# Half units of weight sums moved on GpSimd, rows of x loaded later, in the mixing blocks of a one-core encoder layer

## The reference

```
xn = rmsnorm(x, g);  z = xn @ w_in                 # q | k | v | x branch | gate
attn = banded attention over 64-token chunks       # q, k, v; window 128, learned sinks
lru  = gelu(gate) * scan(conv(x branch))           # gated linear recurrence over time
h    = x + concat(attn, lru) @ w_out               # end of the mixing half
y    = h + relu(rmsnorm(h) @ w_up)^2 @ w_down      # MLP, hidden width 4096
out  = rmsnorm(y)                                  # and the caches and states of k, v, conv, lru
```

## Time and profile before

| what | value |
|---|---|
| median of the runs | 2216.5 us (2215.3 to 2217.7) |
| the profiled execution, its span | 2212.88 us, 2211.1 us |
| PE, busy | 1985.6 us (90%) |
| DVE, busy | 1535.7 us (69%) |
| ACT, busy | 1014.1 us (46%) |
| POOL, busy | 500.7 us (23%) |
| DMA | 500.91 MB, mean 227 GB/s |

### The profile page before, as it was taken

The page is one execution under the profiler, slowest core; times in us unless marked ns, Lnnn a source line. Parts: engine busy times, 40 slices in busy tenths (PEclk is TensorE's granted clock), DMA queues, the critical chain, the costliest instruction groups (busy, mean ns, idle before and its releaser), DMA issues.

```text
span 2211.1 us, 34222 instructions
## 1 busy us (share of the span) xinstructions
PE 1985.6 (90%) x11669; PEld 1882.8 (85%) x11669; DVE 1535.7 (69%) x2167; ACT 1014.1 (46%) x1967; POOL 500.7 (23%) x411
## 2 busy tenths in 40 slices
PE   6779789789789669999999889999999789999994
PEld 5678578578578569999999879999999789999994
DVE  7767667667668677888887866666666766666663
ACT  5555345454454435555555544433334534434431
POOL 3436456456549230100000400100001300000000
PEclk9989899899899889999999999999999999999997
DMA  5757566666566459998998977778878677777771
GB/s 173 232 157 228 168 195 217 176 210 194 175 202 189 127 197 301 316 308 273 338 340 295 314 242 240 238 209 250 269 230 252 222 223 217 219 216 216 216 215 63
DMA packets 396538, 500.91 MB, mean 227 GB/s; under 512 B 27498, under 2 KB 301450, under 8 KB 396394
## 3 DMA queue, kind: packets, MB, share of 16 engines
q1 hardware_dynamic: 394698, 493.38, 72.1%
q0 software_dynamic: 1696, 5.67, 0.7%
HBM read 375.36 MB, written 123.68 MB: 226 GB/s over the span
## 4 chain that ended last, share of the span: by engine, by line
PE 65%; DVE 10%; issue 9%; POOL 7%; DMA 4%; ACT 3%; SPq 1%; POOLq 0%; DVEq 0%; ACTq 0%
PE results L2067 20%; PE scores_a L2067 13%; PE tail L2067 13%; PE results L1851 10%; PE aux L2067 8%; DVE w_lo L1401 2%; PE aux L1971 1%; POOL prob L961 1%; DMA s_scratch<-w_hi 1%; POOL xrow L932 1%; POOL xrow L930 1%; DVE xg_lo L1411 1%; POOL xrow L934 1%; DVE av L1560 1%; POOL xrow L936 1%
## 5 line engine op out<-in xcount | busy, mean ns | idle before, releaser
L1083 ACT ACTIVATE w_hi<-w_raw 128x512 fp32r<-128x512 f32 (+1 forms) x360 | 240.6, 690 | 394.8 <-PE results L2067 169.6
L1526 DVE TENSOR_TENSOR w_lo<-w_raw,w_hi 128x512 fp32r<-128x512 f32 (+1 forms) x360 | 292.4, 826 | 50.7 <-ACT w_hi L1083 50.5
L1851 PE MATMUL results<-xg_hi,w_hi 128*128 128x448 f32 (+1 forms) x560 | 211.4, 377 | 30.6 <-DVE w_lo L1401 21.2
L1851 PE MATMUL results<-xg_hi,w_lo 128*128 128x448 f32 (+1 forms) x560 | 201.1, 359 | 0.0
L1851 PE MATMUL results<-xg_lo,w_hi 128*128 128x448 f32 (+1 forms) x560 | 200.9, 359 | 0.0
L2067 PE MATMUL results<-hn_hi,w_hi 128*128 128x348 f32 x576 | 188.2, 327 | 13.4 <-DVE hcur L1736 7.8
L1401 DVE TENSOR_TENSOR w_lo<-raw,w_hi 128x1024 fp32r<-128x1024 f32 x110 | 158.1, 1437 | 58.8 <-ACT w_hi L1019 58.5
L1019 ACT ACTIVATE w_hi<-raw 128x1024 fp32r<-128x1024 f32 x110 | 116.2, 1056 | 162.9 <-PE results L1851 158.2
L2067 PE MATMUL results<-hn_hi,w_lo 128*128 128x348 f32 x576 | 186.5, 324 | 0.0
L2067 PE MATMUL results<-hn_lo,w_hi 128*128 128x348 f32 x576 | 186.4, 324 | 0.0
L2067 PE MATMUL scores_a<-hn_hi,w_hi 128*128 128x348 f32 x480 | 156.2, 325 | 4.7 <-DVE hn_lo L1516 2.9
(11 more groups left out here) (275 smaller groups left out, 5723.8 us busy)
## 6 DMA issues: line engine op xcount, KB each, us to landing
w_lo<-s_scratch SPq DMA_DIRECT2D x128, 512.0 KB, 4.5
w_hi<-s_scratch SPq DMA_DIRECT2D x256, 256.0 KB, 3.5
w_raw<-in_w_up SPq DMA_DIRECT2D x144, 256.0 KB, 4.6
w_raw<-in_w_down SPq DMA_DIRECT2D x144, 256.0 KB, 4.3
raw<-in_w_in SPq DMA_DIRECT2D x70, 512.0 KB, 5.0
w_raw<-s_raw SPq DMA_DIRECT2D x64, 512.0 KB, 5.5
s_scratch<-w_lo SPq DMA_DIRECT2D x64, 512.0 KB, 6.0
s_scratch<-w_hi SPq DMA_DIRECT2D x128, 256.0 KB, 6.1
```

Of the source, the lines that this page charges most:

```text
L1083: nc.scalar.activation(ring(w2_hi, u, ks[0], len(ks)), raw_slots(u, ks[0], len(ks)), ACT.Copy)\
L1526: nc.vector.tensor_tensor(w2_lo[u.s][:, PHYS[ks[0]]:PHYS[ks[0]] + len(ks), :], raw_slots(u, ks[0], len(ks)), ring(w2_hi.bitcast(F32), u, k ...
L1851: last = nc.tensor.matmul(out, wt, x(kx), start=(start and i == 0 and part == 0), stop=(stop and i == len(ks) - 1 and part == 2))
```

## The change

Two things, in the mixing blocks. In SP's loop, `load_x` for the next block moves from n = 16 to n = 18, and at that step it now comes behind `move_sums`. It holds for the first block and the three middle ones. In the middle blocks' `SUM_MADE`, half unit 9 moves from "scan" to behind the probabilities of round 0, half unit 10 from round 1 to round 2; half unit 14 moves from ahead of the adds of squares to behind the second of them, half unit 15 from behind the third to behind the fifth. No instruction is added or removed.

```diff
-            "mid": {"start": (0, 1, 2), "ix0": (3, 4), "ix1": (5, 6), "scan": (7, 8, 9), 1: (10,), 3: (11,), 5: (12,), 6: (13,),
-                    "squares": (14,), "squares3": (15,)},
+            "mid": {"start": (0, 1, 2), "ix0": (3, 4), "ix1": (5, 6), "scan": (7, 8), 0: (9,), 2: (10,), 3: (11,), 5: (12,), 6: (13,),
+                    "squares2": (14,), "squares5": (15,)},
...
-                    if nxt and q == 7:
+                    move_sums(blk, n)
+                    if nxt and q == 8:
                         sp.wait_ge(mixed, blk.before(2) + 2)
                         sp.wait_ge(freed, 2 + uses + Z1)
                         for r in range(4):
                             load_x(nxt, r)
-                    move_sums(blk, n)
...
-                make_sums(blk, "squares")
                 for c in range(1, KT):
                     add_square(blk.next(), c)
-                    if c == 3:
-                        make_sums(blk, "squares3")
+                    make_sums(blk, f"squares{c}")
```

## The result

The changed kernel takes 2178.85 us (2178.8 and 2178.9) against 2216.5: ratio 0.983, 95% interval 0.981 to 0.986, 37.7 us less. The two profiled executions (2212.88 and 2178.8 us) differ by 34.1 us: that of before lies 3.6 us under its median. What follows splits these 34.1.

What follows compares the result with a forecast made beforehand. PE, the busiest engine, was held by GpSimd's `prob`, queued behind half unit 10's late load; 36 - 1 + 3 + 7 + 0 = 45 us off the median of 2216.5 gave 2171 us, range 2157 to 2191.

Steps and rivals of the forecast that it cites:

- Half unit 10 and x: 36: Middle blocks, rounds 1 to 4: PE's wait for GpSimd's `prob` goes, 12 us a block, 36 us for three.
- the whole 12 us go: Middle blocks: the 12 us a block lost around PE's wait for `prob` all vanish, with 1.4 us to spare.
- Half unit 9: -1 and +3: Three middle blocks: half unit 9 behind round 0's `prob` costs 1 us; DVE's faster `rt` and `mix_lo` win 3.
- the first rival: Middle blocks: half unit 9 disturbs the softmax, round 1's `prob` some 2 us late; 36 us won, 2180 us; chance 0.15.
- the rival's rule: DVE with two SBUF inputs contends with GpSimd; three softmax steps could each lose an add, 0.72 us, 2.2 a block.
- The first block: +7: First block: x moved away lets a half unit's load land earlier; of 12.3 us wait 5.5 stay, 7 won, bounds 5 to 12.3.
- Cost 0, with 4 us to spare: Later issue of x: first tile lands near 429, PE needs it at 433.1, so no cost.
- x later in the middle blocks: 0: x issued at n = 18, from about 425, still lands before PE's transposition; cost 0 us.
- The fourth rival: x lands too late, behind its transposition, in all four blocks: at 450, 23 us slower, 2240 us; chance 0.02.
- The second: Rival: half unit 10 still lands late, wait moves to round 3; 21 us won, 2195 us; chance 0.08.
- The tail: 0: Middle blocks' end, half units 14 and 15 between the adds: between +3 and -1 us a block, taken as 0.
- the third rival: Middle blocks' end: adds end with the last square, each wins 3 us; 54 us in all, 2162 us; chance 0.13.

## Why the prediction held, point by point

It said 2171 us, 45 us off; 37.7 came by the medians and 34.1 in the two traces, with the range holding. The mechanism was right, and the sum 11 us too high against its own execution. By stretches of the traces, the 34.1 are: rounds 0 to 5 of three middle blocks +36.0, from round 5 to x -4.0, x to the sum +2.6, sum to round 0 -1.8, first block +3.8, last block and MLP -2.5. The last of these lies ahead of the last block's round 0 (102.0 us from its sum against 99.6); its cause stays open, since kernels whose sum is waited for took 101.3 to 103.0 there, but so did one without that wait (102.5). Behind that round the two traces agree within 0.1 us, and by the scatter of that stretch this is luck.

*Half unit 10 and x: 36.* Exactly 36.0 up to round 5. The step that failed stands behind it: "the whole 12 us go". I checked the half units next to the stall, and put half unit 13's load at nought, but not half unit 12, which stands between the `prob`s of rounds 5 and 6. Without the stall the rounds come at their own pace, and its load and adds hold round 6: 1.3 us in each block, 4.0 of the 36 given back. That this half unit does it is shown by its move, and by x at n = 17, which made its wait longer. It does not do it alone: half unit 9's new place has used up the slack, as its move back shows.

*Half unit 9: -1 and +3.* The net of 2 is not shown. The +3 is of the right kind: from `rt` to round 0 the changed kernel is 1.2 us faster than before over the three blocks, and 2.3 faster than with the half unit back. The -1 was looked for in the wrong place: round 1's `prob` transposition follows round 0's without a wait, so the first rival fell, but the rounds behind start later, and 3.0 of the 4.0 us in round 6 come back when the half unit does. DVE's step with the sink took 0.66 us beside it (0.16 with the half unit back beside the scan), one step of the three. It began at 390.22, while an add of the half unit ran, and ended with that add, at 390.88 against 390.86. So it lost 0.5 us, the rest of one add, and not the three whole adds of 0.72 each that the rival's rule allowed. The rule of the Trainium skill, "SBUF — State Buffer", "Who interferes with whom", agrees with the trace in that, and in which pairs meet, 1.09 against 1.61 and 0.16 against 0.66, while its worst case did not occur here. The price of 0.5 us an instruction was read too high from the earlier trace rows: there three instructions lost 1.06 us together.

*The first block: +7.* It gave 3.8, under the lower bound of 5, though by less than the scatter of a first block. PE's wait for `prob` fell from 12.3 to 4.1, so the rounds behind it came 7.6 to 8.5 us earlier, more than the term assumed. The step that failed is the next one: "Cost 0, with 4 us to spare" was worked out in a middle block and taken for all four. In the first, with five rounds instead of seven, x was issued at 115.73 and PE wanted it at 120.7; it came 1.2 us late and PE ran on at a granted clock of 0.70 for 5.5 us. With x a step earlier the first sum came 3.4 us sooner, which brings the term to 7.2.

*x later in the middle blocks: 0.* Right: 3.7 us to spare for the 4 forecast, and one step later there is a wait. The fourth rival falls with it. The second falls by GpSimd's rows: half unit 10 does not wait, and PE's round 3 does not either.

*The tail: 0.* Right in size and in form: `hacc` is no longer waited for, the sum is, and the matmuls run slower behind it. Taking it back changed nothing that the times or the blocks show. What I did not see is that 13 us lay there: the third rival asked whether the adds could end with the last square, and they can, once both half units stand behind them.

*The signs.* Three of those that the prediction named went against it. A wait for `prob` of over 1 us is left in the middle blocks, in round 6 and not in round 3, where it was looked for. A wait for x, which was to show that the prediction is wrong, is there in the first block. The middle blocks became 12.7, 11.9 and 8.3 us shorter, not 14 to 15. Others held: half unit 10 does not wait, x is issued 7.7 us ahead of its transposition, and a wait stands ahead of the sum in place of the one for `hacc`.

The result, 1.7% faster, lies in the case to which the chances gave 0.51, with that for over 2% close beside it at 0.47: as the text said, the forecast stood almost on the boundary.

## What to carry to other kernels

Where an engine does side work between steps of the critical chain, put that work behind the last step that something waits for, not at even distances; and look at what its load stands behind on the queue, since each of the two was worth half here. After removing a stall, go through every later place where the side work still stands between two such steps: with the stall gone, the slack that it gave them is gone too. And side work that no step directly behind it waits for can still cost a later one, as half unit 9 did in round 6. A margin worked out in the loop's body has to be worked out again for the first block, which has fewer rounds.

## What the runs showed that was not expected

A short wait can cost PE several times its length through the clock, and not each time. With x at n = 19, middle block 3 had waits of 1.29 and 0.90 us, then 0.54 for 10.9 us, and was 4.9 us longer than in the changed kernel. Block 1 had nearly the same two (1.28 and 0.86), but 0.86 over the 12 us behind them, and was 2.9 us longer:

```profile
270.00:282.00 12.00, 10.82 (x63) 9.60 (x64) 2.90 (x4) 4.99 (x10) 1.63 (x3) 0.86 0.73 196
```

In the changed kernel the wait of 1.28 us alone, in round 6 of each middle block, left the clock at 1.00. What tells blocks 1 and 3 apart was not tested.
